# Stick-breaking attention regrouped from 32 units of 128 to 512 columns into 20 units of 512

## The reference

```python
def stick_breaking_attention(q, k, v):
    """q, k, v: [B, H, S, Dh]. A[t,s] = beta_ts * prod_{s<j<t}(1-beta_tj), s<t."""
    ...
        causal = kpos[None, :] < qpos[:, None]
        z = jnp.einsum('bhqd,bhkd->bhqk', q_blk, k).astype(jnp.float32) * scale
        log_beta = jax.nn.log_sigmoid(z)
        log_one_minus = jnp.where(causal, jax.nn.log_sigmoid(-z), 0.0)
        suffix = lax.cumsum(log_one_minus, axis=3, reverse=True) - log_one_minus
        w = jnp.where(causal, jnp.exp(log_beta + suffix), 0.0)
        return jnp.einsum('bhqk,bhkd->bhqd', w.astype(v.dtype), v)
```

## Time and profile before

| what | value |
|---|---|
| runs | 3303.46, 3307.32 and 3308.29, median 3307.32 |
| span of the profiled execution | 3301.8 |
| TensorE matmul busy | 3209.7 (97% of the span), 15400 instructions |
| VectorE, ScalarE, GpSimd busy | 2030.7, 1317.5, 1393.4 |
| attention, from the end of `v_lo` to the end of the last value product | 1846.8 to 1943.5, 96.7 |

### The profile page before, as it was taken

How to read it: one execution, slowest core, us unless ns; L and a number is a source line. 1 busy time by engine, 2 the same in 40 slices (tenths; PEclk the granted TensorE clock), 3 DMA queues, 4 the chain that set the end, 5 groups by cost and what they waited for, 6 DMA issues and landing times. The chain is left out here.

```text
span 3301.8 us, 45138 instructions
## 1 busy us (share of the span) xinstructions
PE 3209.7 (97%) x15400; PEld 2748.8 (83%) x15400; DVE 2030.7 (62%) x3076; ACT 1317.5 (40%) x2032; POOL 1393.4 (42%) x694
## 2 busy tenths in 40 slices
PE   6999999999999999999999889999999899999999
PEld 4888888888888888888887667999989898888887
DVE  6553476513653164411248778888869596888887
ACT  3232343224322232322234663244848483333333
POOL 3454435444544444444445334466533343223221
PEclk9999999999999999999999899999999999999999
DMA  6554335532654222222322103355898989999997
GB/s 257 191 197 154 115 124 202 197 102 88 210 197 139 96 91 97 90 98 94 109 83 79 37 33 109 102 175 167 291 364 274 361 281 329 350 343 346 347 343 262
DMA packets 219996, 620.72 MB, mean 188 GB/s; under 512 B 22624, under 2 KB 88416, under 8 KB 217312
## 3 DMA queue, kind: packets, MB, share of 16 engines
q1 hardware_dynamic: 89296, 324.76, 28.9%
q10 hardware_dynamic: 93712, 160.11, 13.8%
q0 software_dynamic: 36864, 134.23, 11.5%
HBM read 572.88 MB, written 46.14 MB: 187 GB/s over the span
## 5 line engine op out<-in xcount | busy, mean ns | idle before, releaser
L537 POOL TENSOR_TENSOR wlo<-raw,whi 128x1024 fp32r<-128x1024 f32 x394 | 1022.2, 2597 | 1180.4 <-ACT whi L585 1179.8
L1764 PE MATMUL bank<-hhi,whi 128*128 128x512 f32 (+1 forms) x2672 | 992.1, 371 | 2.2 <-POOL wlo L537 1.5
L585 ACT ACTIVATE whi<-raw 128x1024 fp32r<-128x1024 f32 x599 | 631.9, 1058 | 884.5 <-PE bank L1766 533.6
L1766 PE MATMUL bank<-hhi,wlo 128*128 128x512 f32 (+1 forms) x2672 | 984.4, 368 | 0.0
L1765 PE MATMUL bank<-hlo,whi 128*128 128x512 f32 (+1 forms) x2672 | 984.4, 368 | 0.0
L1764 PEld LDWEIGHTS bank<-hhi,whi 128*128 128x128 f32 x2672 | 502.7, 188 | 68.9 <-issue 3.9
L1765 PEld LDWEIGHTS bank<-hlo,whi 128*128 128x128 f32 x2672 | 502.5, 188 | 65.1 <-issue 1.2
L1766 PEld LDWEIGHTS bank<-hhi,wlo 128*128 128x128 f32 x2672 | 502.2, 188 | 64.9
L1070 DVE CUSTOM_DVE_ANT_0 ada_raw<-ada_raw,cond_row 128x1024 f32<-128x1024 f32 x128 | 304.6, 2411 | 158.5 <-DMA ada_raw<-ada_dram 158.4
L1595 DVE TENSOR_TENSOR wlo<-raw,whi 128x1024 fp32r<-128x1024 f32 x205 | 250.7, 1223 | 126.5 <-ACT whi L585 126.2
L2223 PE MATMUL bank<-whi,we 128*128 128x512 f32 x768 | 300.0, 391 | 4.3 <-ACT act_out L949 4.3
(11 more groups left out here) (350 smaller groups left out, 4147.4 us busy)
## 6 DMA issues: line engine op xcount, KB each, us to landing
raw<-stream_dram SPq DMA_DIRECT2D x599, 512.0 KB, 3.3
ada_raw<-ada_dram ACTq DMA_DIRECT2D x128, 512.0 KB, 4.1
expert_acts<-act_out ACTq DMA_DIRECT2D x128, 192.0 KB, 4.6
act_in<-expert_acts ACTq DMA_DIRECT2D x128, 192.0 KB, 6.2
expert_weights<-spread ACTq DMA_DIRECT2D x16, 1024.0 KB, 12.1
g_ring<-expert_weights ACTq DMA_DIRECT2D x128, 128.0 KB, 5.4
first_raw<-ada_dram SPq DMA_DIRECT2D x8, 1024.0 KB, 18.2
x<-xin_dram ACTq DMA_DIRECT2D x1, 2048.0 KB, 5.2
```

The source lines that it names most:

```text
L537: pool.tensor_tensor(wlo[:, s, :, :], raw[:, s, :, :], whi[:, s, :, :].bitcast(F32), ALU.subtract).then_inc(lo_ready, 1)
L585: act.activation(whi[:, s, :, :], raw[:, s, :, :], ACT.Copy).then_inc(hi_ready, 1)
L1764: pe.matmul(bank, whi[:, s, b, :], rhi, start=start, stop=False)
L1766: return pe.matmul(bank, wlo[:, s, b, :], rhi, start=False, stop=stop)
```

## The change

Both heads of a pair are cut into five units that each fill a bank of 512 columns: two "outer" units (key blocks 1 and 3 of one head, 384 + 128 columns), one "middle" unit (key block 2 of both heads, 256 + 256), two "whole" units (key block 0 of one head). That gives 20 units. Other edits:

- The -1e30 above the diagonal is added in `scores` (`far_diagonal`), before Abs. Softplus of it is 0, so VectorE's mask product goes away.
- `exponent(u)` waits for `lows_for(u)`: an outer unit also needs the softplus of the middle unit of its pair.
- In a middle unit the second half's scores wait for the first half's (`half_scored`).
- `LAG` is 4; `ZN` stays 5. The weights of unit u-5 are then made by ScalarE in its round u-1.
- The v product writes banks 0, 1, 6, 7 and no longer waits for the gates, which are read from banks 2 to 5. `scores(0)` and `scores(1)` go to banks 2 and 3 and don't wait for `v_lo`; `scores(2)` does.
- `sum_out(6)` stands before the last value product.
- `w_lo` on GpSimd and all ScalarE and VectorE steps work on 512 columns.

```diff
-OUT_AT = {2: 4, 5: 5, 8: 6, 11: 7, 17: 0, 25: 1}
-LAG = 3
-Z_BANK = (0, 1, 2, 3, 6)
+OUT_AT = {1: 4, 3: 5, 5: 6, 7: 7, 12: 0, 17: 1}
+LAG = 4
+Z_BANK = (2, 3, 0, 1, 6)
+V_BANK = (0, 1, 6, 7)
 ZN = len(Z_BANK)
-MEAN_COPY_AT = 15
+MEAN_COPY_AT = 10
...
-ATT_OFF = [0, 512, 896, 1152]
-ATT_COLS = 1280
+AB_COLS = 768
+AB_OFF = {1: (0, 384), 3: (384, 512), 2: (512, 768)}
...
-UNITS = [(h, i) for h in range(HEADS) for i in reversed(range(CT))]
+UNITS = []
+for _h in range(0, HEADS, 2):
+    UNITS += [("outer", ((_h, 1, 0), (_h, 3, 384))), ("outer", ((_h + 1, 1, 0), (_h + 1, 3, 384))),
+              ("middle", ((_h, 2, 0), (_h + 1, 2, 256))),
+              ("whole", ((_h, 0, 0),)), ("whole", ((_h + 1, 0, 0),))]
+PAIR = 5
+LAST_OF_HEAD = {_h: PAIR * (_h // 2) + 3 + _h % 2 for _h in range(HEADS)}
+TAKE_AT = {LAST_OF_HEAD[_h] + LAG + 2: _h for _h in range(HEADS)}
+def lows_for(u):
+    return PAIR * (u // PAIR) + max(u % PAIR, 2) + 1
...
+    ab_hi = [place(f"ab_hi{a}", at_kb, [P, 2, AB_COLS], F32R) for a, at_kb in enumerate((80, 88))]
+    ab_lo = [place(f"ab_lo{a}", at_kb, [P, 2, AB_COLS], F32R) for a, at_kb in enumerate((168, 174))]
+    whole_hi = place("whole_hi", 180, [P, 2, T], F32R)
+    whole_lo = place("whole_lo", 184, [P, 2, T], F32R)
...
-                if u == len(UNITS) - 2:
+                if u == len(UNITS) - 3:
...
+                dve.scalar_tensor_tensor(buf, psum[Z_BANK[u % ZN]][:, :], 0.0, buf, ALU.max, ALU.add).then_inc(sp_ready, 1)
+                dve.wait_ge(sp_ready, u + 1)
+                a = h // 2 % 2
+                if kind == "outer":
+                    hi, lo = (z[:, h % 2, 0:T] for z in (ab_hi[a], ab_lo[a]))
+                elif kind == "middle":
+                    buf = buf.rearrange("p (a n) -> p a n", a=2)
+                    hi, lo = (z[:, :, T:AB_COLS] for z in (ab_hi[a], ab_lo[a]))
+                else:
+                    hi, lo = (z[:, h % 2, :] for z in (whole_hi, whole_lo))
...
-            pe.wait_ge(gates_ready, 2 * CT)
-            pe.wait_ge(gelu_ready, 2)
+            pe.wait_ge(gelu_ready, CT)
...
             def scores(u):
-                h, i = UNITS[u]
-                n = T - P * i
                 if u >= ZN:
                     pe.wait_ge(w32_ready, u - ZN + 1)
-                r, t = slice(64 * (h % 2), 64 * (h % 2) + 64), h // 2
-                out = psum[Z_BANK[u % ZN]][:, 0:n]
-                kc, qc = slice(P * i, P * i + P), slice(P * i, T)
-                pe.matmul(out, k_hi[r, t, kc], q_hi[r, t, qc], start=True, stop=False)
-                pe.matmul(out, k_hi[r, t, kc], q_lo[r, t, qc], start=False, stop=False)
-                pe.matmul(out, k_lo[r, t, kc], q_hi[r, t, qc], start=False, stop=True).then_inc(z_ready, 1)
+                elif u == 2:
+                    pe.wait_ge(v_ready, CT)
+                bank = psum[Z_BANK[u % ZN]]
+                for p, (h, i, off) in enumerate(UNITS[u][1]):
+                    r, t = slice(64 * (h % 2), 64 * (h % 2) + 64), h // 2
+                    out = bank[:, off:off + T - P * i]
+                    kc, qc = slice(P * i, P * i + P), slice(P * i, T)
+                    if p == 1 and UNITS[u][0] == "middle":
+                        pe.wait_ge(half_scored, u // PAIR + 1)
+                    pe.matmul(out, k_hi[r, t, kc], q_hi[r, t, qc], start=p == 0, stop=False, skip_group_check=True)
+                    pe.matmul(out, k_hi[r, t, kc], q_lo[r, t, qc], start=False, stop=False, skip_group_check=True)
+                    mm = pe.matmul(out, k_lo[r, t, kc], q_hi[r, t, qc], start=False, stop=False, skip_group_check=True)
+                    if p == 0 and UNITS[u][0] == "middle":
+                        mm.then_inc(half_scored, 1)
+                        far_diagonal(bank, UNITS[u][1])
+                if UNITS[u][0] != "middle":
+                    mm = far_diagonal(bank, UNITS[u][1])
+                mm.then_inc(z_ready, 1)
+            def far_diagonal(bank, parts):
+                for _, _, off in parts:
+                    mm = pe.matmul(bank[:, off:off + P], sq_round[:, IDENT_R, :], sq_round[:, FAR, :],
+                                   start=False, stop=False, skip_group_check=True)
+                return mm
...
             def exponent(u):
-                h, i = UNITS[u]
-                pe.wait_ge(l_ready, u + 1)
-                for j in range(i, CT):
-                    off = P * (j - i)
-                    n = T - P * j
-                    out = psum[Z_BANK[u % ZN]][:, off:off + n]
-                    for part in (l_hi, l_lo):
-                        pe.matmul(out, sq_round[:, TRI if j == i else ONES, :], part[:, h % 2, ATT_OFF[j]:ATT_OFF[j] + n],
-                                  start=False, stop=False, skip_group_check=True)
-                pe.matmul(psum[Z_BANK[u % ZN]][:, 0:P], sq_round[:, IDENT_R, :], sq_round[:, FAR, :],
-                          start=False, stop=True, skip_group_check=True).then_inc(expo_ready, 1)
+                pe.wait_ge(l_ready, lows_for(u))
+                for h, i, off in UNITS[u][1]:
+                    for j in range(i, CT):
+                        out = psum[Z_BANK[u % ZN]][:, off + P * (j - i):off + T - P * i]
+                        for part in softplus(h, j):
+                            mm = pe.matmul(out, sq_round[:, TRI if j == i else ONES, :], part,
+                                           start=False, stop=j == CT - 1, skip_group_check=True)
+                mm.then_inc(expo_ready, 1)
...
             pe.wait_ge(q_ready, 2 * CT)
             pe.wait_ge(const2_ready, 1)
-            pe.wait_ge(v_ready, CT)
-            pe.wait_ge(gelu_ready, CT)
+            pe.wait_ge(gates_ready, 2 * CT)
...
-            sum_out(KT - 2)
+                if u == len(UNITS) + LAG - 1:
+                    sum_out(KT - 2)
```

More of the change, by code:

```diff
@@ L554, in _ @@
             lo_range(SEG["gr"][0] + KT, SEG["mix_out"][0] + LOOK)
-            for u, (h, i) in enumerate(UNITS):
-                n = T - P * i
+            for u in range(len(UNITS)):
                 pool.wait_ge(w32_ready, u + 1)
-                pool.tensor_tensor(w_lo[:, u % 2, 0:n], w32[:, u % 2, 0:n], w_hi[:, u % 2, 0:n].bitcast(F32), ALU.subtract).then_inc(w_ready, 1)
+                pool.tensor_tensor(w_lo[:, u % 2, :], w32[:, u % 2, :], w_hi[:, u % 2, :].bitcast(F32), ALU.subtract).then_inc(w_ready, 1)
             lo_range(SEG["mix_out"][0] + LOOK, SEG["up"][0] + LOOK + LEAD_AT[TT])
@@ L849, in _ @@
             for c in range(CT):
[L850 removed]
+                act.activation(v_hi[:, c, :], psum[V_BANK[c]][:, :], ACT.Copy).then_inc(vhi_ready, 1)
             act.preload_act_table_set("natural_log_exp_and_others")
@@ L860, in weights @@
                     act.wait_ge(pv_done, u - 1)
-                act.activation(w_hi[:, u % 2, 0:n], psum[Z_BANK[u % ZN]][:, 0:n], ACT.Exp)
+                act.activation(w_hi[:, u % 2, :], psum[Z_BANK[u % ZN]][:, :], ACT.Exp)
                 if u >= 2:
                     act.wait_ge(w_ready, u - 1)
-                act.activation(w32[:, u % 2, 0:n], psum[Z_BANK[u % ZN]][:, 0:n], ACT.Exp).then_inc(w32_ready, 1)
+                act.activation(w32[:, u % 2, :], psum[Z_BANK[u % ZN]][:, :], ACT.Exp).then_inc(w32_ready, 1)
             def square_out(j):
@@ L1493, in _ @@
                 dve.wait_ge(lhi_ready, u + 1)
-                dve.tensor_tensor(l_lo[:, h % 2, cols], buf, l_hi[:, h % 2, cols].bitcast(F32), ALU.subtract).then_inc(l_ready, 1)
-            for u in range(len(UNITS) - LAG, len(UNITS)):
-                split_w(u)
-            take_o(HEADS - 1)
+                dve.tensor_tensor(lo, buf, hi.bitcast(F32), ALU.subtract).then_inc(l_ready, 1)
+            for u in sorted(TAKE_AT):
+                if u >= len(UNITS):
+                    take_o(TAKE_AT[u])
@@ L2022, in _ @@
                         cols = slice(st * P, st * P + P)
-                        pe.matmul(psum[st][:, :], hhi[:, k, cols], rh, start=k == 0, stop=False)
-                        pe.matmul(psum[st][:, :], hlo[:, k, cols], rh, start=False, stop=False)
-                        mm = pe.matmul(psum[st][:, :], hhi[:, k, cols], rl, start=False, stop=k == KT - 1)
+                        out = psum[V_BANK[st]][:, :]
+                        pe.matmul(out, hhi[:, k, cols], rh, start=k == 0, stop=False)
@@ new lines, in scores, with softplus @@
+                if UNITS[u][0] != "middle":
[6 more added lines that the diff above has]
+                return mm
+            def softplus(h, j):
+                if j == 0:
+                    return whole_hi[:, h % 2, :], whole_lo[:, h % 2, :]
+                first, last = AB_OFF[j]
+                return ab_hi[h // 2 % 2][:, h % 2, first:last], ab_lo[h // 2 % 2][:, h % 2, first:last]
@@ L2055, in weighted @@
             def weighted(u):
-                h, i = UNITS[u]
-                n = T - P * i
+                kind, parts = UNITS[u]
                 pe.wait_ge(w_ready, u + 1)
-                if i == CT - 1 and h >= 2:
```

(16 more changed lines are left out.)

48 lines of the change are left out of this document (19 added, 29 removed).

## The result

The changed kernel takes 3288.91 us, median of 4 runs (3286.20 to 3292.30). The kernel before takes 3305.39 beside it, median of 4 (3301.01 to 3308.29). The ratio is 0.9948, interval 0.9936 to 0.9959: 16.5 us or 0.5% faster. The profiled execution took 3286.20 with a span of 3284.4, against a span of 3301.8 before. TensorE's matmul time fell from 3209.7 to 3193.7.

The account below looks back on a forecast made before the run. TensorE's own list was taken to bound attention, its first quarter at half clock. A gain of 14.5 us at full clock less 5.3 for half clock left 9.2: span 3301.8 to 3292.6, plus 5.5 gives 3298.1 us; range 3291 to 3309.

Parts of the forecast that it names:

- I take the rise at 1871, as before: Early attention: TensorE's clock returns from half to full at 1871, leaving 12.7 us of half clock after the first `w32`.
- the clock's term: Rounds after 1858.3: each us at half clock loses 0.42 us, so 12.7 us lose 5.3.
- The head: Attention's start: `v_lo` comes no earlier, TensorE's list runs at half clock from 1847.1 to 1857.0, first `w32` at 1858.3.
- the softplus is ready before its turn: Ahead of exponent(0): unit 2's softplus ends on VectorE about 1853.5, before the exponent's turn at 1854.8.
- The rounds: Attention's units at full clock: 18.4 us per pair of heads, plus 2.75 for sums between w32(0) and w32(15).
- The hand-over back: From ScalarE's `w32` to TensorE's next scores: between nothing and 0.27 us, taken as 0.10.
- the twenty hand-overs: Each unit's bank passing from TensorE through ScalarE's `w_hi` and `w32` and back: 1.29 us each.
- The ring: Each round: scores, exponent, hand-over, `w_hi`, `w32`, hand-over back in series, as scores(u) waits for `w32` of unit u-5; 1.29 us hand-over.
- What follows attention: Output projection and retrieval: in series with the same work, so attention's gain reaches the end unchanged.
- Rival 2: Attention's start: the clock rises earlier or does not fall; gain 12 to 16 us, 3291 to 3295.5; chance 0.17.
- Rival 3: Rounds: hand-overs of 1.8 add 10 us, or the clock rises only from 1877 to 1900; 3300.7 to 3312; chance 0.31.
- Rival 4: Rounds: the ring's gaps keep or bring back half clock; 3314 or more, or 3309 to 3314; chance 0.10.

Follow-up runs that it names:

- after_keep: Changed kernel plus unread TensorE products in three waits: 32 for `v_lo`, 5 ahead of exponent(0), 5 ahead of scores(5); 3284.98 us, ratio 0.9935.
- after_old_v: Changed kernel with the value product put back in banks 0 to 3 behind its old waits, the first scores behind it; 3295.15 us, ratio 0.9967.
- after_warm: Changed kernel plus 32 unread products of 512 columns and 128 rows in TensorE's wait for `v_lo`; 3287.90 us, ratio 0.9938.
- after_both: Changed kernel with ScalarE reading the bank once (`w_hi` copied from `w32`) and unread products in three waits (32, 5, 3); 3278.82 us, ratio 0.9919.
- after_hand: Changed kernel with one more 512-column exponential on ScalarE between `w_hi` and `w32` of each unit; 3303.62 us, ratio 0.9986.
- before_again2: Kernel before, unchanged, run again for another profiled execution; 3304.37 us.
- after_again2: Changed kernel, unchanged, run again for another profiled execution; the two such repeats took 3289.97 and 3286.75 us.

## Why the prediction was wrong, and where it was right

**The step that failed** is "I take the rise at 1871, as before": 12.7 us of half clock behind the first `w32`. Measured are 6.1 (1856.19 to 1862.24), 6.7 and 7.1. The price beside it was right. From the first `w32`'s end to the start of the last value product the changed kernel needs 71.2 us with 6.1 of half clock, and after_keep 68.5 with none: 0.44 us per us (0.46 by each of the other two executions), where the prediction worked out 0.42. So the clock's term, 5.3 in the forecast, measures 71.2 - 68.5 = 2.7, which is 2.6 us less. The argument for 1871 was a list of what TensorE did before it rose, 3.4 us without a gap. But TensorE had 16 us without a gap there, from 1854.54 to 1870.50, which the prediction overlooked. It also took the half clock to begin "as before". In the changed kernel TensorE ran out of work sooner and the clock fell sooner, ahead of `v_lo`'s end, where half clock costs little (in after_keep the whole head at 1.00 gains 1.4 us). The rest, a half clock 3.4 us shorter or more, stays open: no run shows what in the changed list ends it. Shown is that the rises of the two kernels lie apart, 16.5 to 17.6 against 24.0 to 24.5 in three executions each.

**The head** (from `v_lo`'s end to the first `w32`) was read almost right. `v_lo`'s end does not move with the v product by more than it scatters (means of 1847.11 before and 1846.76 after): costing that at nothing was right for `v_lo`, but not for the clock. Exponent(0) came at 1852.95 and the first `w32` 10.5 us behind `v_lo`, where 11.5 was forecast. That is 1.0 us more of gain. The v product's new place with the two early scores is worth 4.9 us of the stage, by after_old_v. The early scores were inside the forecast's list, but not named as a term. At full clock the 4.6 us that the list saves between `v_lo` and `w32` are not to be had: after_keep gains 1.4 there, since the first exponent then has to wait for `ab_lo` (1.34 us in after_warm). The sentence that the softplus is ready before its turn holds at half clock only.

**The rounds** hold. A pair takes 19.2 and 18.9 us at full clock, where 18.4 with 0.9 of sums was forecast. The hand-over back is 0.05 and not 0.10, and the twenty hand-overs of the changed kernel measure 1.24 to 1.44 in the forecast's terms, 1.29 there. The sum from the first `w32` to the last value product at full clock, 69.4, measures 68.5. The ring is a real cost: 3.0 us of it go when ScalarE reads the bank once (after_both against after_keep).

**What follows attention** is not "the same work" in time: it is 1.1 us shorter in each of three executions (19.3, 19.4, 19.2 before; 18.1, 18.2, 18.2 after, from the last value product's end to `m_lo`'s start). VectorE's four steps account for it: they take 3.90, 3.98 and 3.75 us before and 2.74 in each execution after, and start 9.45 us behind the last value product's end in both kernels. They no longer meet GpSimd's subtraction. That this is the reason is argued from the rows above; no run moved one of them alone. This is a second term that the prediction put at nothing.

**The sum.** The forecast gain was 9.2. The stage's start-to-start forecast, 86.2, came out at 81.7, 4.5 less: 2.6 for the clock, 1.0 for the head and 0.9 in rounds that were a little cheaper. That makes 13.7 up to the start of the last value product. Its group then takes 0.98 us and not 1.30, since in the kernel before the clock fell inside it (1942.7), and 1.1 more come behind attention: 15.1 in all. Means over three executions: 13.8 in the stage, end to end, 1.1 behind it, 0.4 from `v_lo`'s end and 0.9 in the rest, together 16.2 of span. The last two are within the scatter: the executions of the changed kernel differ by 3.8 us in span.

**The rivals.** Rival 2, a rise that comes earlier, is what happened, and past its own 12 to 16 us. It got 0.17 because activity had not raised the clock before; the same fact had been taken as a constant in the forecast. Rival 3 fails: no hand-over is near 1.8. Rival 4 did not happen, but after_hand shows how near it lay. With waits of 0.3 to 0.6 us a unit (and one of 0.96) the clock stays at 1.00 for 65 us; in after_hand, with waits of 0.8 to 0.9 among them, it falls three times in 25 us, and most of the gain is gone. The Trainium skill ("TensorE: Matmul & The Clock Gate", "A second HAM failure mode: psum-queue depth-cycling") says that short idle spells between groups make the clock go back and forth. The changed kernel does not bear it out, and after_hand does.

## What to carry to other kernels

Take the moment at which a clock rises from a fixed place in the program only if the work around that place stays the same; when the list changes, work the forecast out for an early and a late end. When an edit lengthens or fills one wait, look for the next wait of the same engine: the three fills together gained 4.1 us in the stage, the first alone 1.7. And where two engines pass a bank back and forth, let the first step that reads it be the last one: here that cost ScalarE nothing (0.63 us for 0.60) and took 2 to 3 us off the stage.

## What the runs showed of the hardware

- At 0.50, TensorE worked for 16.32 us without a gap before the clock rose (before_again2), and for 6.56 (after_again2). The Trainium skill ("TensorE: Matmul & The Clock Gate", "What's actually happening") says that activity releases the throttle; the first of these rows is activity that long did not.
- In the kernel before, a wait of 1.41 us for `w_lo` was followed by a fall of the clock in each of three executions (at 1901.7, 1902.6 and 1901.8), while the second such wait, 22 us later, was not, and the third, of 1.95 us, was again (at 1942.7, 1943.6 and 1942.8). In after_both two waits of 0.8 us, 18 us apart, were followed by no fall; in after_hand waits of 0.8 to 0.9 some 10 us apart were followed by three.
- A rounding copy of 128x512 from one buffer to another on ScalarE takes as long as the exponential out of a bank: 0.63 against 0.60 us.
